# Two products of a transformer MLP by one level of Strassen's method, in two phases

## The reference, cut to what matters

```
def squared_relu_mlp(h, w_up, w_down):
    a = jax.nn.relu(h @ w_up)
    return (a * a) @ w_down

h = h + mix
h = h + squared_relu_mlp(rms_norm(h, mlp_norm[i]), mlp_w_up[i], mlp_w_down[i])
return rms_norm(h, final_norm)
```

## Time and the profile before

| what | value |
|---|---|
| median of 3 runs | 2297.77 us (2296.86 to 2298.41) |
| span of the profiled execution | 2296.6 us |
| time around the span (median less span) | 1.2 us |
| PE busy, share of the span | 97% |
| DVE, ACT, POOL busy | 63%, 42%, 9% |

### The profile page before, as it was taken

One profiled execution on the slowest core, in us unless ns is written; L12 is line 12 of the kernel. 1 busy time (PEld: TensorE's weight loads), 2 busy tenths in 40 slices (PEclk: granted clock), 3 DMA queues, 4 the chain that ended last, 5 costly groups with the idle time before them and its releaser, 6 DMA issues.

```text
span 2296.6 us, 27818 instructions
## 1 busy us (share of the span) xinstructions
PE 2222.8 (97%) x11316; PEld 1856.7 (81%) x11316; DVE 1450.6 (63%) x2316; ACT 971.2 (42%) x1521; POOL 214.8 (9%) x316
## 2 busy tenths in 40 slices
PE   8999999999999999999999999999998999899997
...
GB/s 146 47 79 122 195 46 61 81 138 87 98 137 92 101 133 97 110 102 67 54 79 92 35 45 88 28 1 1 1 1 42 256 55 102 299 393 386 386 379 225
DMA packets 79872, 280.64 MB, mean 122 GB/s; under 512 B 9936, under 2 KB 10224, under 8 KB 78592
## 3 DMA queue, kind: packets, MB, share of 16 engines
...
## 4 chain that ended last, share of the span: by engine, by line
PE 86%; DVE 7%; ACT 4%; issue 1%; DMA 1%; POOLq 0%; SPq 0%; ACTq 0%; DVEq 0%
PE psum L98 26%; PE psum L100 25%; PE psum L99 25%; PE psum L2471 2%; PE psum L2482 2%; ACT MP_hi L2572 1%; PE psum L978 1%; DVE MP_lo L2665 1%; ACT PB L2538 1%; DVE small L2618 1%; PE psum L951 1%; PE psum L3309 1%; PE psum L3038 1%; DVE idx L3011 1%; DVE cur L3014 0%
## 5 line engine op out<-in xcount | busy, mean ns | idle before, releaser
L98 PE MATMUL psum<-U_hi,w_hi 128*128 128x512 f32 x688 | 271.0, 394 | 13.4 <-DVE w_lo L243 10.7
L234 ACT ACTIVATE w_hi<-raw 128x1024 fp32r<-128x1024 f32 (+2 forms) x163 | 162.7, 1002 | 280.5 <-PE psum L100 267.7
L99 PE MATMUL psum<-U_lo,w_hi 128*128 128x512 f32 x688 | 269.0, 391 | 0.0
L100 PE MATMUL psum<-U_hi,w_lo 128*128 128x512 f32 x688 | 268.7, 391 | 0.0
L243 DVE TENSOR_TENSOR w_lo<-raw,w_hi 128x1024 fp32r<-128x1024 f32 (+2 forms) x162 | 187.9, 1167 | 113.3 <-ACT w_hi L234 113.1
L98 PE MATMUL psum<-W_hi,w_hi 128*128 128x512 f32 x512 | 199.7, 390 | 0.9 <-DVE X L1092 0.9
L100 PE MATMUL psum<-W_hi,w_lo 128*128 128x512 f32 x512 | 199.2, 389 | 0.0
L99 PE MATMUL psum<-W_lo,w_hi 128*128 128x512 f32 x512 | 199.2, 389 | 0.0
L98 PE MATMUL psum<-a_hi,w_hi 128*128 128x512 f32 x512 | 199.2, 389 | 0.0
L99 PE MATMUL psum<-a_lo,w_hi 128*128 128x512 f32 x512 | 199.2, 389 | 0.0
L100 PE MATMUL psum<-a_hi,w_lo 128*128 128x512 f32 x512 | 199.2, 389 | 0.0
...
## 6 DMA issues: line engine op xcount, KB each, us to landing
rawe<-in_w_e SPq DMA_DIRECT2D x112, 512.0 KB, 16.9
mraw<-in_w_mod POOLq DMA_DIRECT2D x128, 256.0 KB, 3.0
rawx<-in_w_e SPq DMA_DIRECT2D x56, 512.0 KB, 18.0
raw<-in_w_up SPq DMA_DIRECT2D x32, 512.0 KB, 3.6
raw<-in_w_dn SPq DMA_DIRECT2D x32, 512.0 KB, 3.6
raw<-in_w_e SPq DMA_DIRECT2D x24, 512.0 KB, 17.0
X<-in_xT SPq DMA_DIRECT2D x8, 512.0 KB, 9.4
raw<-in_w_q SPq DMA_DIRECT2D x8, 512.0 KB, 4.9
```

What stands on the lines that cost most here:

```text
L98: e.matmul(o, l[0], r[0], start=first, stop=False, skip_group_check=skip)
L99: e.matmul(o, l[0], r[1], start=False, stop=False, skip_group_check=skip)
L100: return e.matmul(o, l[1], r[0], start=False, stop=last, skip_group_check=skip)
L234: act.e.activation(hi, src, ACT.Copy).then_inc(w_hi, 1)
```

## The change

Each product is cut into 2 x 2 blocks and done with Strassen's seven block products in place of eight. M1 to M7 are numbered as usual: with weights W and inputs B, M1 = (W11+W22)(B11+B22), M2 = (W21+W22)B11, M3 = W11(B12-B22), M4 = W22(B21-B11), M5 = (W11+W12)B22, M6 = (W21-W11)(B11+B12), M7 = (W12-W22)(B21+B22). The code's `FIRST`, `THEN` and `PASSES` are orders of these numbers. The inputs' two row halves are channels, their column halves tokens.

**Up.** The seven sums of the input B are made once and kept in `B_OP`, split. Their making begins in `so_*` (`hi2`, `sum6`, `hi5`) and most of it lies behind the last `so` product: VectorE's `sum1`, `lo1`, `sum3`, `lo3`, `lo7`, `lo4`, POOL's `sum7`, `sum4`. Then 16 groups g, each of 7 passes of 4 mm3. A group takes four tiles UA (512 wide), UC, UB, UD (1024), of which POOL adds or subtracts three out of two raw tiles (`tA`, `tC`, `tB`). The outputs are combined by ACT (copies m1, m5, m2), POOL (q, s) and VectorE (v2, v1, c22, c11, relus r12, r22, r21, r11), squared by ACT (a12, a22, a21, a11), and then combined into the seven sums that the second product needs (VectorE t6, t1, t3, POOL t4, t7). SyncE stores those in device memory (`ta`, 7 x 8 x 128 x 1024). Four banks serve a group, and the other four the next. In iteration g each engine's list first ends group g-1, and then makes the tiles of the next group between the middle steps of group g.

**Down.** 7 passes of 8 steps; a step takes one tile of weights S (POOL adds or subtracts two raw tiles in five of the seven passes) and one of `ta`, and does 4 blocks d of 2 mm3. VectorE adds or subtracts each bank into one or two parts of X, which was stored before the stage and is loaded again. Tiles are made 3 steps ahead.

The modulation loads move from POOL's queue to SyncE's; 60 of its pieces are used in up, four to a group from group 1 on, and 36 (68 multiply-and-sums) in steps 6 to 45 of down. The sums of squares for the final norm are made half by half. The host reorders w_up and w_dn to suit. Much of the diff is bookkeeping of buffers; its core:

```diff
+    FIRST, THEN = (2, 6, 5, 1, 3, 7, 4), (1, 6, 5, 2, 7, 3, 4)
+    BANK = {1: 0, 7: 0, 6: 1, 5: 2, 3: 2, 2: 3, 4: 3}
+    ONTO = {7: "m1", 3: "m5", 4: "m2"}
...
+        T_UA.append(sum_tile(zA[:] if g else w_raw[2][:, 0:512], (ml.pool("tA", g),), ml.pe("u", g, 1), 0, 512))
+        T_UC.append(sum_tile(w_raw[2][:], (ml.pool("tC", g),), ml.pe("u", g, 2 if g else 5), 1))
+        T_UB.append(sum_tile(R1[g].buf(), (ml.pool("tB", g, 1),), ml.pe("u", g, 7), 2))
+        T_UD.append(sum_tile(R0[g].buf(), (R0[g].landed(),), ml.pe("u", g, 4), 3))
...
+    OPERAND = {1: (T_UA, 0), 2: (T_UC, 1), 3: (T_UD, 0), 4: (T_UD, 1), 5: (T_UC, 0), 6: (T_UB, 1), 7: (T_UB, 0)}
...
+    PASSES = (1, 2, 3, 5, 6, 4, 7)
+    A_OF = {1: (0, 3, ALU.add), 2: (2, 3, ALU.add), 3: (0, None, None), 4: (3, None, None), 5: (0, 1, ALU.add),
+            6: (2, 0, ALU.subtract), 7: (1, 3, ALU.subtract)}
+    TO = {1: ((0, 0, 1), (1, 1, 1)), 2: ((1, 0, 1), (1, 1, -1)), 3: ((0, 1, 1), (1, 1, 1)),
+          5: ((0, 0, -1), (0, 1, 1)), 6: ((1, 1, 1),), 4: ((0, 0, 1), (1, 0, 1)), 7: ((0, 0, 1),)}
+    AHEAD = 3
...
+        T_S.append(sum_tile(S_X[s].buf(), (S_X[s].landed() if y is None else ml.pool("S", s),), step_done(s),
+                            S_PLACES[s % 4]))
+        T_T.append(sum_tile(S_T[s].buf(), (S_T[s].landed(),), step_done(s), T_PLACES[s % 4]))
...
+            e.scalar_tensor_tensor(B_SUM[1][:, k, :], X[:, 4 + k, half(1)], G2[:, 4 + k:5 + k], X[:, k, half(0)],
+                                   ALU.mult, ALU.add).then_inc(*so.dve.one("sum1", k))
...
+            e.scalar_tensor_tensor(B_SUM[3][:, k, :], X[:, 4 + k, half(1)], G2[:, 4 + k:5 + k], X[:, k, half(1)],
+                                   ALU.mult, ALU.subtract).then_inc(*so.dve.one("sum3", k))
...
+    def make_ta(pool, g, to):
+        pool.wait_ge(*R0[g].landed())
+        r = R0[g].buf()
+        pool.e.tensor_tensor(to, r[:, half(0)], r[:, half(1)], ALU.add).then_inc(*ml.pool.one("tA", g))
+    def make_tc(pool, g):
+        pool.wait_ge(*R0[g].landed())
+        pool.wait_ge(*R1[g].landed())
+        pool.e.tensor_tensor(w_raw[2][:], R0[g].buf(), R1[g].buf(), ALU.add).then_inc(*ml.pool.one("tC", g))
+    def make_tb(pool, g):
+        pool.wait_ge(*ml.pool("tC", g))
...
+            pool.e.tensor_tensor(R1[g].buf()[:, half(i)], R1[g].buf()[:, half(i)], R0[g].buf()[:, half(1 - i)],
+                                 ALU.subtract).then_inc(*ml.pool.one("tB", g, i))
...
+    def up_pool(pool):
+        e = pool.e
+        for g in range(N_G):
+            if g < N_G - 1:
+                if g:
+                    pool.wait_ge(*lo_mark(T_UA[g]))
...
+                make_ta(pool, g + 1, zA[:])
+            else:
+                down_sum(pool, 0)
+            if g:
+                up_ends_pool(pool, g - 1)
+            if g < N_G - 1:
+                pool.wait_ge(*lo_mark(T_UC[g]))
+                make_tc(pool, g + 1)
+                make_tb(pool, g + 1)
+            else:
+                down_sum(pool, 1)
+                down_sum(pool, 2)
+            c = cbuf[g % 2]
+            pool.wait_ge(*ml.act("m5", g))
+            pool.wait_ge(*ml.act("m2", g))
+            e.tensor_tensor(c[2][:], c[2][:], c[1][:], ALU.add).then_inc(*ml.pool.one("q", g))
+            pool.wait_ge(*ml.act("m1", g))
+            pool.wait_ge(*ml.pool("q", g))
+            e.tensor_tensor(c[0][:], c[0][:], c[2][:], ALU.subtract).then_inc(*ml.pool.one("s", g))
+    def up_ends_pool(pool, g):
+        c = cbuf[g % 2]
+        pool.wait_ge(*ml.act("a21", g))
+        pool.wait_ge(*ml.act("a11", g))
...
+        pool.e.tensor_tensor(rg[2][:], c[3][:], c[2][:], ALU.subtract).then_inc(*ml.pool.one("t4", g))
+        pool.wait_ge(*ml.act("a22", g))
+        pool.wait_ge(*ml.pool("t4", g))
+        pool.e.tensor_tensor(c[3][:], c[3][:], c[0][:], ALU.add).then_inc(*ml.pool.one("t7", g))
...
+        for g in range(N_G):
+            if g:
+                up_ends_act(act, g - 1)
+                make_hi(act, T_UD[g])
...
+                m1(g)
+                make_hi(act, T_UA[g + 1] if g < N_G - 1 else T_T[0])
+                m5(g)
+                m2(g)
+                make_hi(act, T_UC[g + 1] if g < N_G - 1 else T_T[1])
+                make_hi(act, T_UB[g + 1] if g < N_G - 1 else T_T[2])
...
+    def up_ends_act(act, g):
+        c = cbuf[g % 2]
+        for what, i, r in (("a21", 3, "r21"), ("a11", 2, "r11")):
+            act.wait_ge(*ml.dve(r, g))
+            act.e.activation(c[i][:], c[i][:], ACT.Square).then_inc(*ml.act.one(what, g))
...
+    def up_dve(dve):
+        e = dve.e
+        for g in range(N_G):
+            c, z = cbuf[g % 2], g % 2
+            if g:
+                up_ends_dve(dve, g - 1)
+                make_lo(dve, T_UA[g + 1] if g < N_G - 1 else T_T[0])
+                for i in up_mods(g):
+                    n = i - 32
+                    dve.wait_ge(*mraw_in[n % 4].at(n // 4 + 1))
+                    dve.wait_ge(*ml.act("silu", 0))
+                    mod_step(dve, 0, i, mraw[n % 4], srow, mraw[n % 4])
+                make_lo(dve, T_UC[g + 1] if g < N_G - 1 else T_T[1])
...
+                for k in range(4):
+                    dve.wait_ge(*so.act("hi7", k))
+                    e.scalar_tensor_tensor(B_OP[7][1][:, k, :], B_SUM[7][:, k, :], G2[:, 4 + k:5 + k],
+                                           f(B_OP[7][0][:, k, :]), ALU.mult, ALU.subtract).then_inc(
+                                               *so.dve.one("lo7", k))
+                for k in range(4):
+                    split_sum(dve, 4, k)
+                make_lo(dve, T_UA[1])
+                nm2.inverse(dve, 0)
+                make_lo(dve, T_UC[1])
+                nm2.inverse(dve, 1)
+            dve.wait_ge(*ml.pool("s", g))
+            dve.wait_ge(*ml.pe("u", g, 6))
+            e.tensor_tensor(c[0][:], bank(up_bank(g, 6)), c[0][:], ALU.add).then_inc(*ml.dve.one("v2", g))
+            dve.wait_ge(*ml.pe("u", g, 7))
+            e.tensor_tensor(c[2][:], bank(up_bank(g, 7)), c[2][:], ALU.subtract).then_inc(*ml.dve.one("v1", g))
+            make_lo(dve, T_UB[g + 1] if g < N_G - 1 else T_T[2])
+            dve.wait_ge(*ml.pe("u", g, 3))
+            dve.wait_ge(*ml.dve("v2", g))
+            e.tensor_tensor(c[0][:], bank(up_bank(g, 3)), c[0][:], ALU.add).then_inc(*ml.dve.one("c22", g))
+            dve.wait_ge(*so.dve("n2", "inv", 1))
+            dve.wait_ge(*ml.pool("q", g))
+            relu(dve, c[1], bank(up_bank(g, 3)), 1, "r12", g)
+            dve.wait_ge(*ml.dve("c22", g))
+            relu(dve, c[0], c[0][:], 1, "r22", g)
+    def relu(dve, to, x, h, what, g):
+        dve.e.scalar_tensor_tensor(to[:], x, 0.0, R2[:, half(h)], ALU.max, ALU.mult).then_inc(*ml.dve.one(what, g))
+    def up_ends_dve(dve, g):
+        c, e = cbuf[g % 2], dve.e
+        dve.wait_ge(*ml.pe("u", g, 4))
...
+        relu(dve, c[3], bank(up_bank(g, 4)), 0, "r21", g)
+        dve.wait_ge(*ml.dve("v1", g))
+        e.tensor_tensor(c[2][:], bank(up_bank(g, 4)), c[2][:], ALU.add).then_inc(*ml.dve.one("c11", g))
+        dve.wait_ge(*ml.dve("c11", g))
+        relu(dve, c[2], c[2][:], 0, "r11", g)
+        make_lo(dve, T_UD[g + 1] if g < N_G - 1 else T_T[2])
...
+        dve.wait_ge(*ml.act("a12", g))
+        dve.wait_ge(*ml.act("a22", g))
+        dve.wait_ge(*ml.act("a11", g))
...
+        e.tensor_tensor(rg[1][:], c[2][:], c[1][:], ALU.add).then_inc(*ml.dve.one("t6", g))
...
+        e.tensor_tensor(rg[0][:], c[2][:], c[0][:], ALU.add).then_inc(*ml.dve.one("t1", g))
+        dve.wait_ge(*ml.dve("t6", g))
+        e.tensor_tensor(c[1][:], c[1][:], c[0][:], ALU.subtract).then_inc(*ml.dve.one("t3", g))
...
+    def up_pe(pe):
+        for g in range(N_G):
+            for i in THEN if g else FIRST:
+                b, (ts, h) = up_bank(g, i), OPERAND[i]
+                w = use(pe, ts[g])
+                if i in ONTO:
+                    pe.wait_ge(*ml.act(ONTO[i], g))
...
+                for k in range(4):
+                    if g == 0:
+                        pe.wait_ge(*so.dve(f"lo{i}", k))
+                    m = mm3(pe.e, bank(b), cols([x[:, half(h)] for x in w], k, 128), ch(B_OP[i], k, 0, 512),
+                            k == 0 and i not in ONTO, k == 3, True)
+                m.then_inc(*ml.pe.one("u", g, i))
...
+            hand_over(up_bank(g, 1), 1, ml.dve("v1", g))
+            hand_over(up_bank(g, 6), 1, ml.dve("v2", g))
+            hand_over(up_bank(g, 3), 1, ml.dve("c22", g), ml.dve("r12", g))
+            hand_over(up_bank(g, 4), 1, ml.dve("r21", g), ml.dve("c11", g))
...
+    def stores(sp, g):
+        c = cbuf[g % 2]
+        store(sp, g, 5, c[0], ml.act("a22", g))
+        store(sp, g, 2, c[2], ml.act("a11", g))
+        store(sp, g, 6, rg[1], ml.dve("t6", g))
+        store(sp, g, 1, rg[0], ml.dve("t1", g))
+        store(sp, g, 3, c[1], ml.dve("t3", g))
+        store(sp, g, 4, rg[2], ml.pool("t4", g))
+        store(sp, g, 7, c[3], ml.pool("t7", g))
...
+    def down_sum(pool, s):
```

(83 more changed lines are left out.)

776 lines of the change are left out of this document (495 added, 281 removed).

## The result

The changed kernel took **2357.7 us** (median of 4 runs, 2356.65 to 2359.98) beside 2297.3 us for the kernel before on the same chip: ratio 1.0264, 95% interval 1.0252 to 1.0277. It is 60 us slower; 2307 had been forecast, and the range ended at 2326. The profiled execution took 2356.65 us with a span of 2354.8.

What follows compares the result with a forecast made beforehand. TensorE was taken to bound the kernel before; afterwards engine turns would set up's pace. Start 42, ring 336, passes 16.3, clock 3, handover 6 and down 304.7 made 708.0 against 699.2: 2307 us, range 2258 to 2326.

Steps and rivals of the forecast that it cites:

- 87.0 us of matmuls less: MLP on TensorE: seven eighths of 3072 matmuls remain, 384 fewer at 0.2267 us each, 87.0 us less.
- The two take turns: Up: VectorE instructions with two SBUF inputs and POOL's SBUF reads exclude each other; data together 18.7 us a group.
- Prices: POOL's additions, extrapolated from narrower ones in the profile: 1.30 us for 512 wide, 2.44 us for 1024.
- The ring of 24.0 us: Up: cycle from POOL's `s` through VectorE's v2 to the next group's, 24.0 us a group, 14 turns, 336 us.
- Start 42: MLP start, from the last `so` product until `lo` of UB(1): 42 us, bounds 29.5 and 44.2.
- Six passes and clock, 19.3: End of up: six passes of 2.72 us, 16.3, plus 3 us for TensorE's half clock on the last group.
- Down "at its matmuls": Down: costed at TensorE's matmuls alone, 56 steps of 5.44 us, 304.7 us, with TensorE always busy.
- asked for about six steps ahead: Down: three loads of 512 KB in each 5.44 us step, issued about six steps before use.
- Landing 3.6 us: Down: each 512 KB load lands in 3.6 us.
- Handover 6: Down's first steps: POOL's S for step 3 stands behind t4, t7 of group 15, coming some 6 us late.
- Tail 0, within 2: End of the MLP: last adds, squares and sums stay as they are, 0 us, within 2 either way.
- (3): Down: three-step lead doesn't absorb VectorE's blocked steps; 17 us more, 2324; chance 0.14.

## Why the prediction was wrong

By its own steps, with what was measured:

- *87.0 us of matmuls less*: 384 fewer, at 0.2267 us each. Right.
- *The two take turns*: right, and the profile's own narrow rows had shown it. *Prices*: 1.30 and 2.44 us against 1.26 and 2.34 measured.
- *The ring of 24.0 us*: 23.15 us. The size held, and so did the order of limits; 14 turns 324.1 us, not 336. The part that came out differently is the last: in the turn shown tA waits for its raw load (2.33 us) until the multiply-and-sums are past, so that it holds none of them. But the ring is no chain of waits: VectorE works through its list with 1.65 us of idle time a turn, and what the order of POOL's list decides is how many of its instructions are held. Later edits took that down in parts: without t4 and t7 ahead of `s` the turn is 21.7 us, without the late raw load 20.6, and with one multiply-and-sum less 19.1, where TensorE is the bound.
- *Start 42*: `lo` of UB(1) ended at 388.9, 46.8 us after the start, above both bounds (44.2 was the upper); what fills the last 2.6 us wasn't tested. *Six passes and clock, 19.3*: 18.3 (712.9 to 731.2); the rows that the 3 us of clock were taken from show it fallen behind small products with waits of 1.3 us and less, not behind 5 us.
- *Down "at its matmuls"*, 304.7: 364.4 with the handover's waits in it, against 304.7 and 6. **This is the step that failed**, by 53.7 us; up was 8 us shorter than forecast. The sentence "asked for about six steps ahead" took the distance of the raw buffers (three steps) and of the tiles (three more) for that of the loads. And "moving 60 mod loads behind them there delays nothing" speaks of the loads of up; the 36 row loads that down has in the same list, among its tile loads, have no term at all. In the list of step s each of them waits for the row four back, which VectorE uses in step s - 4 or s - 5 of its own list. A tile load of step s + 1 stands behind it, and VectorE wants that sum in step s - 2 of its list, so only one or two of its steps lie between. In the wait shown above it wanted the sum at 934.2, 3.6 us after the row, and had it at 940.77, 10.1 us after: 6.6 for issue and landing, 2.4 for POOL, 1.1 for ACT. VectorE's next row stands behind that `lo`, so the delay is passed on. Moving the rows two steps back gave 36 us, and taking their waits away with their loads gave 34.
- *Landing 3.6 us*: 5.8 to 6.4 with 254 to 319 GB/s under way; the 3.6 had been read at 106 GB/s. How much of the loss is due to this alone wasn't tested; with the rows later in the list loads under 304 GB/s cost TensorE nothing behind 810 us.
- *Handover 6*: 12.2 us of waits. The larger part, 8.56, is the one forecast, POOL's sum of step 3 behind t4 and t7 of group 15, only longer; the other, 3.59, follows from a load that came 9.18 us late for POOL, at 415 GB/s, and had no term.
- *Tail 0, within 2*: the first product of the next stage comes 14.7 us after the last of the MLP instead of 12.6, 2.1 more.
- Rivals: (3) named "Down is late too" and 17 us, from VectorE falling behind. Down was late, by 53.7 us, but by another mechanism: VectorE had only 33 and 44 us of work in 60 when TensorE waited. A loss by the order of SyncE's list was not among the cases, so the range was too short at its upper end.
